# A two-block transformer on one NeuronCore: modulation products with the operands swapped, moved from the heads of the first block into its MLPs, and column pieces of the second block's products issued side by side

## What is computed

```python
def first_block(x, ...):
    for l in range(2):
        u = rms_norm(h, attn_norm[l])
        proj = u @ w_in[l]                     # 34 column chunks for heads, 24 for gates
        a, r, c = differential_attention(...), bidirectional_retention(...), grouped_query_attention(...)
        merged = sum(sigmoid(gate_logits) * (branch @ w_branch[l, n]) for n, branch in enumerate((a, r, c)))
        h = h + merged @ w_out[l]
        h = h + square(relu(rms_norm(h, mlp_norm[l]) @ w_mlp_in[l])) @ w_mlp_out[l]

def second_block(x, c, ctx, c_ctx, w_mod, b_mod, ...):
    for l in range(2):
        mx = split(silu(c) @ w_mod[l] + b_mod[l], 6)         # w_mod[l] is 1024 x 6144
        mc = split(silu(c_ctx) @ w_mod[l] + b_mod[l], 6)
        # modulated norm, w_in, Fourier / MLA / convolution mixer, w_o, modulated norm, MLP
```

## Time and profile before

| | |
|---|---|
| median of 3 runs | 4130.52 us (4129.41 to 4133.31) |
| the profiled execution's own time | 4130.38 us |
| its span | 4128.6 us |
| mean granted TensorE clock | 0.955 of full speed |
| PE, DVE, ACT busy | 94%, 42%, 37% |
| transfers | 303.37 MB, mean 73 GB/s |

### The profile page before, as it was taken

One profiled execution on the slowest core, in us unless ns is written; L12 is line 12 of the kernel. 1 busy time (PEld: TensorE's weight loads), 2 busy tenths in 40 slices (PEclk: granted clock), 3 DMA queues, 4 the chain that ended last, 5 costly groups with the idle time before them and its releaser, 6 DMA issues.

```text
span 4128.6 us, 45135 instructions
## 1 busy us (share of the span) xinstructions
PE 3891.5 (94%) x16959; PEld 2860.4 (69%) x16959; DVE 1744.0 (42%) x2372; ACT 1534.1 (37%) x2269; POOL 2.4 (0%) x9
## 2 busy tenths in 40 slices
PE   7999899999999998999999799988999989989998
PEld 5666678788876665787788574457888876447886
DVE  4565443433355664434333434523222244434333
ACT  4454332333334544323333334423223224433333
POOL 0000000000000000000000000000000000000000
PEclk8999999999999999999999799988999989999999
DMA  4222233233332222333333210001222222002332
GB/s 126 82 81 83 72 92 94 84 92 92 96 97 77 83 76 77 92 95 90 87 94 94 87 51 21 0 26 46 61 62 65 61 64 71 1 20 83 92 92 81
DMA packets 570351, 303.37 MB, mean 73 GB/s; under 512 B 26017, under 2 KB 564977, under 8 KB 570225
## 3 DMA queue, kind: packets, MB, share of 16 engines
q1 hardware_dynamic: 568496, 299.32, 25.1%
q10 hardware_dynamic: 1728, 2.36, 0.2%
HBM read 299.55 MB, written 2.10 MB: 73 GB/s over the span
## 4 chain that ended last, share of the span: by engine, by line
PE 85%; DVE 7%; ACT 3%; DMA 3%; issue 2%; SPq 0%; DVEq 0%; ACTq 0%
PE ps L959 12%; PE ps L960 12%; PE ps L961 12%; PE ps L1134 9%; PE ps L1136 9%; PE ps L1135 9%; PE ps L1304 2%; DMA wraw<-in_w_mod 2%; PE ps L1287 2%; PE ps L1263 2%; PE ps L1077 2%; PE ps L1013 1%; PE ps L1046 1%; PE ps L1011 1%; PE ps L1058 1%
## 5 line engine op out<-in xcount | busy, mean ns | idle before, releaser
L1402 ACT ACTIVATE whi<-wraw 128x1024 fp32r<-128x1024 f32 x544 | 572.1, 1053 | 722.9 <-DMA wraw<-in_w_mlp 256.2
L1859 DVE TENSOR_TENSOR wlo<-wraw,whi 128x1024 fp32r<-128x1024 f32 x544 | 665.1, 1223 | 343.4 <-ACT whi L1402 327.9
L959 PE MATMUL ps<-uhi,whi 128*128 128x512 f32 x1440 | 640.1, 445 | 20.8 <-DVE ulo L1876 20.7
L960 PE MATMUL ps<-ulo,whi 128*128 128x512 f32 x1440 | 582.7, 405 | 0.0
L961 PE MATMUL ps<-uhi,wlo 128*128 128x512 f32 x1440 | 582.2, 404 | 0.0
L1134 PE MATMUL ps<-u2hi,whi 128*128 128x512 f32 (+1 forms) x1024 | 379.0, 370 | 34.2 <-DVE u2lo L2102 32.1
L959 PEld LDWEIGHTS ps<-uhi,whi 128*128 128x128 f32 x1440 | 279.3, 194 | 157.7 <-issue 78.0
L1135 PE MATMUL ps<-u2lo,whi 128*128 128x512 f32 (+1 forms) x1024 | 372.9, 364 | 0.0
L1136 PE MATMUL ps<-u2hi,wlo 128*128 128x512 f32 (+1 forms) x1024 | 372.7, 364 | 0.0
L1134 PE MATMUL ps<-yhi,whi 128*128 128x512 f32 x960 | 345.2, 360 | 5.8 <-DVE ylo L2208 5.8
L1135 PE MATMUL ps<-ylo,whi 128*128 128x512 f32 x960 | 345.0, 359 | 0.0
(11 more groups left out here) (250 smaller groups left out, 5090.8 us busy)
## 6 DMA issues: line engine op xcount, KB each, us to landing
wraw<-in_w_in SPq DMA_DIRECT2D x128, 512.0 KB, 3.9
wraw<-in_w_mlp SPq DMA_DIRECT2D x128, 512.0 KB, 3.9
wraw<-in_w_mod SPq DMA_DIRECT2D x96, 512.0 KB, 4.0
wraw<-in_w_mlp_in SPq DMA_DIRECT2D x64, 512.0 KB, 4.1
wraw<-in_w_mlp_out SPq DMA_DIRECT2D x64, 512.0 KB, 3.8
wraw<-in_w_branch SPq DMA_DIRECT2D x16, 512.0 KB, 3.4
wraw<-in_w_out SPq DMA_DIRECT2D x16, 512.0 KB, 3.8
wraw<-in_w_o SPq DMA_DIRECT2D x16, 512.0 KB, 3.8
```

What stands on the lines that cost most here:

```text
L959: pe.matmul(bank, whs[:, i], x_hi[:, k], start=(i == 0), stop=False)
L960: pe.matmul(bank, whs[:, i], x_lo[:, k], start=False, stop=False)
L1402: act.activation(whi[:, r], wraw[:, r], ACT.Copy).then_inc(w_hi, 1)
L1859: dve.tensor_tensor(wlo[:, r], wraw[:, r], whi[:, r].bitcast(F32), ALU.subtract).then_inc(w_split, 1)
```

## The change

1. No "mod" events in the heads. The 96 chunks are loaded by SP into three places of their own (`mod_raw`), three in every loop turn of four MLP chunks, behind the load of the MLP chunk.
2. The operands change sides: `silu_parts`, now plain fp32 with 32 columns (two used, the rest zero), is the weight operand, and the modulation weights are moved through, 128 columns of plain fp32. The 8 row blocks of a chunk go to four groups of 32 output partitions, two blocks adding up in each. No split by ACT and DVE.
3. PE does such a product after the first, second and third chunk of a loop turn (`mod_product`), and DVE copies the 128 x 128 result. After the fourth, PE transposes three results (`mod_turn`) and DVE adds the four parts into `mod`.
4. `wide_chunk_product` issues the 512 and the 256 column pieces of one row block side by side.
5. Ahead of the output projection of the second block, the wait is put on row blocks 5, 6 and 7 of the first chunk, those that need the late tiles. One PE wait in the mixer that others cover goes, and POOL waits for the last `mod_turn`.

```diff
-    for i, end in enumerate(ends):
-        for c in range(MOD_COLS * i // len(ends), MOD_COLS * (i + 1) // len(ends)):
-            put(end - 0.9, "mod", layer=layer, column=c)
...
-        silu_parts = sb("silu_parts", [P, KT, 4], F32R)
+        silu_parts = sb("silu_parts", [P, KT, 32])
...
+        mod_raw = sb("mod_raw", [P, MOD_GROUP, KT, P], scope=merge_scope)
+        mod_rows = sb("mod_rows", [P, MOD_GROUP * P], scope=merge_scope)
...
+                                if w_mod is not None and n:
+                                    c = P * MOD_GROUP * (2 * KT // RAW * q + i) + P * (MOD_GROUP * KT // RAW * half + n - 1)
+                                    sp.dma_start(mod_raw[:, n - 1], w_mod[:, :, bass.ds(c, P)])\
+                                      .then_inc(mod_in[n - 1], 16)
...
+            def mod_product(b, group):
+
+                pe.wait_ge(mod_in[b], 16 * group + 16)
+                pe.wait_ge(mod_kept, MOD_GROUP * group + (b + 1))
+                for half in range(2):
+                    for lane in range(4):
+                        k = 4 * half + lane
+                        last = pe.matmul(ps[32 * lane:32 * (lane + 1), SCORE + b, 0:P], silu_parts[:, k, :],
+                                         mod_raw[:, b, k], start=(half == 0), stop=(half == 1))
+                last.then_inc(mod_made, 1)
+
+            def mod_turn(group):
+
+                pe.wait_ge(mod_kept, MOD_GROUP * group + 2 * MOD_GROUP)
+                for c in range(MOD_GROUP):
+                    last = pe.transpose(ps[:, ATT, P * c:P * (c + 1)], mod_rows[:, P * c:P * (c + 1)], ident[:, :])
+                last.then_inc(mod_turned, 1)
...
+                                if b < MOD_GROUP:
+                                    mod_product(b, group)
+                                else:
+                                    mod_turn(group)
...
-                for lo, hi in pieces(width):
-                    for k in range(KT):
-                        if split is not None and lo == 0:
-                            pe.wait_ge(lo_ready, split + k + 1)
-                        if ready is not None and lo == 0 and k in ready:
-                            pe.wait_ge(*ready[k])
+                for k in range(KT):
+                    if split is not None:
+                        pe.wait_ge(lo_ready, split + k + 1)
+                    if ready is not None and k in ready:
+                        pe.wait_ge(*ready[k])
+                    for lo, hi in pieces(width):
                         pe.matmul(out[:, lo:hi], whs[:, k], x_hi[:, k, lo:hi], start=(k == 0), stop=False)
+                    for lo, hi in pieces(width):
                         pe.matmul(out[:, lo:hi], whs[:, k], x_lo[:, k, lo:hi], start=False, stop=False)
+                    for lo, hi in pieces(width):
                         last = pe.matmul(out[:, lo:hi], wls[:, k], x_hi[:, k, lo:hi], start=False, stop=(k == KT - 1))
...
-                for b in range(2):
-                    bank_done(pe, bank_evac, s.mixed_tiles - 2 + b)
-                pe.wait_ge(mla_att_free, s.mixed_outs)
+                made = {5: (mla_att_free, s.mixed_outs)}
+                for t in range(2):
+                    n = s.marks["conv_map", t]
+                    made[6 + t] = (bank_evac[n % 2], n // 2 + 1)
...
+                def mods(b, l, group):
+
+                    made = 2 * KT // RAW * QUARTERS * l + group
+                    if b < MOD_GROUP:
+                        dve.wait_ge(mod_made, MOD_GROUP * made + (b + 1))
+                        dve.tensor_copy(mod_rows[:, P * b:P * (b + 1)], ps[:, SCORE + b, 0:P]).then_inc(mod_kept, 1)
+                    else:
+                        dve.wait_ge(mod_turned, made + 1)
+                        parts = ps[:, ATT, 0:MOD_GROUP * P].rearrange("p (c s x) -> p c x s", c=MOD_GROUP, x=32)
+                        dve.tensor_reduce(mod[:, l, bass.ds(MOD_GROUP * group, MOD_GROUP), :], parts[:, :, 0:2, :],
+                                          axis=AX.X, op=ALU.add)
```

More of the change, by code:

```diff
@@ L852, in _ @@
                 for step in s.heads:
-                    if step.name == "mod":
-                        column_chunk(step.chunk, a["w_mod_2"][step.layer], P * step.column)
-                    elif step.name == "part" and step.index == 0:
+                    if step.name == "part" and step.index == 0:
                         whole = step.head
@@ L1002, in _ @@
                             last.then_inc(chunk_done, 1)
[L1003 to L1007, removed]
-                        wls = wlo[:, step.chunk % RAW].rearrange("p (k c) -> p k c", c=P)
-                        for k in range(KT):
-                            pe.matmul(ps[:, step.tile % 2, 0:4], whs[:, k], silu_parts[:, k, :], start=(k == 0),
-                                      stop=False)
-                            last = pe.matmul(ps[:, step.tile % 2, 0:4], wls[:, k], silu_parts[:, k, :],
-                                             start=False, stop=(k == KT - 1))
-                        last.then_inc(chunk_done, 1)
                     elif step.name == "head_norm":
@@ L1123, in _ @@
                                               ready=made if half and b == 0 else None).then_inc(chunk_done, 1)
+                                group = 2 * KT // RAW * q + i + (2 * KT // RAW * QUARTERS * s.layer + KT // RAW * half)
+                                if b < MOD_GROUP:
+                                    mod_product(b, group)
+                                else:
+                                    mod_turn(group)
             def wide_chunk_product(out, slot, x_hi, x_lo, width, split=None, ready=None):
@@ L1344, in _ @@
                         pe.wait_ge(bank_evac[tile % 2], RAW // 2 * i + tile // 2)
-                        wide_chunk_product(ring(tile), chunk % RAW, yhi, ylo, s.width).then_inc(chunk_done, 1)
+                        wide_chunk_product(ring(tile), chunk % RAW, yhi, ylo, s.width,
+                                           ready=None if b else made).then_inc(chunk_done, 1)
                 wide_norm(s.norm2)
@@ L1394, in _ @@
             load_exp_and_log()
-            act.wait_ge(silu_made, 1)
-            act.activation(silu_parts[:, :, 0:2], silu[:, :, :], ACT.Copy).then_inc(silu_hi, 1)
             def weight_hi(chunk, turn=0):
@@ L1925, in _ @@
                             .then_inc(bank_evac[step.tile % 2], 1)
-                    elif step.name == "mod":
-                        lo_before(step.chunk)
-                        dve.wait_ge(chunk_done, step.chunk + 1)
-                        dve.tensor_reduce(mod[:, step.layer, step.column, :],
-                                          ps[:, step.tile % 2, 0:4].rearrange("p (s v) -> p v s", v=2), axis=AX.X,
-                                          op=ALU.add).then_inc(bank_evac[step.tile % 2], 1)
                     elif step.name == "head_scale":
@@ L2065, in quarter @@
                                 .then_inc(m_lo, 1)
+                            mods(b, l, turn + i)
                     total = clear_sum(n, root) if n else None
@@ L2073, in quarter @@
                                 sum_square(n, total, sq, i, b)
+                            mods(b, l, turn + i + KT // RAW)
                 with dve.Fori(0, QUARTERS - 1) as q:
```

28 lines of the change are left out of this document (15 added, 13 removed).

## The result

The changed kernel takes 3915.93 us (median of 4 runs, 3911.92 to 3919.56) where the kernel before took 4131.34 beside it (4 runs, 4129.41 to 4133.31): ratio 0.948, interval 0.946 to 0.950. The forecast was 4019, its range 3952 to 4088: the direction was right, the number is outside the range. The time fell by 215 us where 111 were forecast.

The account below looks back on a forecast made before the run. PE was taken to bound the kernel, with 85% of the chain that ended last. From 4130.4 us: -248 removed from heads, +25 given back, +115 products, +11 transposes, -14 second block, in sum -111: 4019 us, range 3952 to 4088.

Parts of the forecast that it names:

- Given back in the heads: Heads: without modulation chunks filling PE's time during a softmax, PE waits more; 25 us added, between 0 and 60.
- (d): MLPs: the 96 modulation products moved there cost PE 1.2 us each, 115 us added, between 83 and 205.
- (a): Heads: PE no longer does the 96 modulation chunks, 1.785 us each, 171 us removed.
- (b): Heads: half-clock stretches that follow bursts of modulation chunks go; 68 us removed, between 34 and 86.
- (c): Heads: modulation chunk's 4.2 us wait for a PSUM bank, one in each layer, goes; 9 us removed.
- (e): MLPs: PE's transposes of the product results, 0.33 us for three, 32 times; 11 us added.
- (f): MLPs: waits added by the modulation's second load, DVE's copies, the transposes and the silu; nothing.
- (g): Second block: pieces side by side win 3 us behind each of three wide norms, 9 us; nothing in the stream.
- (h): Second block: the 5.8 us wait ahead of the two output projections goes behind ready work; 5 us removed.
- lanes four abreast: Rival, MLP products: four lanes run together, 0.86 us a product, no new waits, most clock back; 3951 us, chance 0.13.
- The softmax chains: Rival, heads: softmax chains bind, 60 us of waits and half the clock's gain lost; 4088 us, chance 0.11.
- the slower case: Rival, MLPs: lanes don't overlap, 2.14 us a product, and the clock falls; +59 us, 4189 us, chance 0.05.

Follow-up runs that it names:

- experiment 2: Kernel before, two versions: modulation matmuls moving 128 columns in place of 4, 4109.0 us; modulation chunks standing singly, no pairs, 4092.95 us.
- Experiment 3: Hollow chunks: kernel before with 2 of the 16 matmuls of each modulation chunk, its load, copy, subtraction, reduction and place kept: 4108.44 us.
- Experiment 1: No modulation: kernel before without any modulation chunk, 3867.66 us; changed kernel without modulation loads, products, transposes and DVE steps, 3829.18 us.
- Experiment 4: Changed kernel with each product's eight matmuls in fewer groups of 32 output partitions: one lane 4039.43 us, two lanes 3955.84 us.

## Why the prediction was wrong

Two steps carried the forecast out of its range. "Given back in the heads" took 25 us of new waits, where the waits of PE fell by 21 us. And (d) took 1.2 us a product, where it is 0.76. Step by step, the forecast against what traces and runs show:

| step | forecast | measured |
|---|---|---|
| (a), (b): PE's work and clock in the heads | -239 | -245 |
| (c) and "Given back in the heads": PE's waits there | +16 | -21 |
| (d) products | +115 | +73 (96 x 0.76) |
| (e) transposes, with (f) | +11 | +8 (rest of 80.5) |
| (g), (h): second block | -14 | -34 |
| sum | -111 | -219 |

- *(a) and (b) held.* Chunk and clock were read rightly, and experiment 2 shows that pairs of thin matmuls did bring the clock down. A us at the low level is worth 0.42 us; at 166 us less of it, (b) is 70, where 68 was taken.
- *"Given back in the heads" failed, by 37 us.* The forecast read the earlier trace rows as a chunk that fills PE's time while the others make a softmax. Experiment 3 shows that this picture is right as long as the chunk's other steps stay: take only its matmuls, and 131 us of waits come. The argument that DVE and ACT have less queued ahead stood in the prediction, as the reason for a low end of 0. But the low end was itself wrong: it left out that waits present now would go too, beyond (c). Experiment 1 shows 64.8 us without work, 21 less than before.
- *(d) failed by 42 us.* It is the size of a term, not its mechanism: 1.2 was chosen "as two is what a row shows", and a row with two lanes doesn't speak against four; a product measures 0.76. Experiment 4 gives the law. The overhead, taken as 0.43 from the earlier trace rows, is 0.33. The product that the rival "lanes four abreast" had, 0.86, was near; its 3951 us was nearest of all cases, and got 0.13.
- *(g) failed where it said "nothing is won in the stream"*: 8 us are, at 0.005 us a pair, too little for two rows rounded to 0.01 us to show; the chunk's start-to-start time does show it. *(h)* held: its waits are 5.8 us, 5 were taken. Together the order (16.5 us of span) and these waits make about 22 of the 34 us. The rest stays open: with the old order the second mixer still is 6 us shorter than before (356.28 against 362.28), and the first varies by 4.7 us between versions that are alike there, since the stretches of low clock fall at other places in each. The PE wait in the mixer that also went was never put back alone.
- *The rivals.* The softmax chains don't bind, and the clock didn't stay low. In the slower case the lanes don't overlap; even that, experiment 4 with one lane, gives 4039 us and not 4189: the clock stays at its full level in the MLPs (in the first one of 475 us its record has one low stretch of 10.2, behind the norm), which is 80 of the difference; the rest are the errors above. What the lanes decide, full or no overlap, is 1.30 us a product or 125 us; experiment 4 gives 124.

The three errors, 37, 42 and 20 us, all have the same sign, so they added up where they might have cancelled. The first two together are enough to leave the range; no single one is.

## What to carry to other kernels

A step's price is not the time of its matmuls. List its bank, its copies and its place in each queue, and ask which of these stay when it moves: here 14 of the 16 matmuls alone were worth 21 us and the whole step 260. Small products of 32 output partitions run four abreast at 0.33 us for each change of form, so put them in groups. Where a stream is re-ordered, look at the clock behind the next norm too. And where two traces differ by a few us of low clock, compare other versions with the same code there before you give the difference to a change.

## What was not expected of the hardware

- Four lanes of 32 output partitions with the same rows overlap fully in fp32: 2.06, 1.19 and 0.76 us for the same eight matmuls in one, two and four lanes.
- The clock stays at its full level but for one stretch through the 48 products of the first MLP, even at 2.06 us each in one lane, while the heads with hollow chunks, where single waits last up to 7 us, have 184 us of half clock, against 22 without chunks.
- Long and short matmuls in turn take 0.347 us a pair, where a run of long and a run of short ones take 0.352.
